# Two transformer blocks in one launch: the opening by channel halves, a new order of panel loads, and block two's side work regrouped among its heads

## The chip, the cores and the metric

One core of one Trainium2 chip runs the whole program in one launch. The metric is the device time in microseconds from the first to the last instruction and what lies around them, as the runs report it; the profile gives the same execution's span. Engines are named as the profile does: PE is the matmul engine (PEld its weight loads), ACT ScalarE, DVE VectorE, POOL GpSimd, SP the engine that only issues DMAs here.

## What is computed

A batch of one, 256 tokens, 1024 channels, float32. The first block:

```python
mod = c @ w_ada + b_ada
shift, scl, gate = split(mod, 3)
h = rms_norm(x, g) * (1 + scl) + shift
u_pool, z_pool, q, k, v, z_attn, m_pool, m_attn = split(h @ w_in)
y_pool = (multiscale_pool(u_pool) * silu(z_pool)) @ w_pool_up
y_attn = (attention(rope(q), rope(k), v) * silu(z_attn)) @ w_attn_up
x = x + gate * ((sigmoid(m_pool) * y_pool + sigmoid(m_attn) * y_attn) @ w_out)
```

The second block takes the normed result. Its modulation (six parts) comes from silu(c_2). It has four retention heads (with a norm over each head and a silu gate), and an attention of eight heads in three branches: over 15 compressed blocks per group of keys and values, over selected blocks, and over a window; each branch is weighted by a sigmoid gate. At 256 tokens the selected and the window branch are two causal softmaxes, so block two has sixteen head passes. The mix goes through w_out_2, and a layer of 16384 small experts (128 x 128 product keys, 16 chosen for each of 8 heads) ends it. With all experts' weights streamed, that layer is 128 panels of `down` and 128 of `up`.

## The kernel before

**Tiles.** Tokens lie in NT = 2 tiles of 128 partitions, channels in C = 8 chunks of 128. A weight panel is 1024 rows by 512 columns, loaded as 128 partitions x 4096 floats in two halves (chunks 0 to 3 and 4 to 7, 1 MB each) into one of SLOTS = 4 slots of SBUF. STREAM (lines 64 to 77) lists the panels in order, each with its user: "pe" panels are multiplied, "dve" panels are modulation columns that DVE sums by itself, "row" is the one modulation panel that PE multiplies as a row. A panel n goes to slot n mod 4, so its load waits until panel n - 4 is used.

**Float32 from three products.** A weight half ("unit", list UNITS, line 90) is split in a high part (ACT's copy to fp32r, `unit_high`, L801, copy at L814) and a low part (POOL's subtraction raw - high, `unit_low`, L735, subtraction at L740, four instructions for a unit; unit 31 alone is DVE's, L1966). The activations are split likewise. PE then adds high x high, low x high and high x low (L1123, L1129, L1135; by rows L1150, L1154, L1163), four matmuls of 512 columns for each token tile in each of the three. HIGH_AT says which of some six places holds the high part of each unit; a place is filled again once the unit before is used.

**Order.** `steps()` (L104) writes out one list of steps, STEPS. Each engine walks through the same list and does its part of each step, so the list's order is the program order of every engine's own queue. POOL is the exception: its units come in the order of UNITS, and the powers for the norms stand between them at fixed places (L757, the retention norm's, behind unit 43). Banks 0 to 3 of PSUM are given out in turn along STEPS (lines 228 to 252); a step that fills a bank waits for the one before to be read.

**Modulation.** A "dve" panel is summed as one `tensor_scalar` (L1663) and seven `scalar_tensor_tensor` (L1665) of 128 x 512, each linked to the one before. Sums with index 0 to 2 (START = 3) accumulate in SBUF (tile tab); those from 3 up to the end of block one accumulate in PSUM and put only the last step in SBUF. PE turns the sum into columns with a product by ones (`start_columns`, L1095, for the first three; L1197 later) or into a row on all partitions for a gate (L1194). DVE's loop sums ahead: behind each "proj" step it does what is due (L2019).

**Opening.** SP loads ada1.2, x, the constants, ada1.3, ada1.0 and ada1.1, then in1.2, the tables and the three broadcast gate rows, then in1.3. DVE sums ada1.2 and ada1.3 (scale), PE makes the row of ada1.0 (`make_row`, L1079, matmuls at L1085), ACT copies it, PE turns it into columns (`row_columns`, L1092), DVE sums ada1.1, and PE turns that into columns. Only when all of scale and shift are there does `mod_ready` rise; then ACT and DVE modulate the four groups of turned chunks (L852, L1735), ACT copies their high parts (L799), DVE subtracts (L1807), and PE starts with in1.2.

**Block one.** Panels in1.4, then 5, 0, 1, 6, 7, 8, 9 one for each attention head; between them score, softmax and product of heads. Then poolup, attnup, out1, and `turn_over(0)` (L138) to block two: the two token tiles are normed, turned and modulated one behind the other, while PE works at out1 and in2.5.

**Block two.** `heads(8, 2 * H, ...)` walks through sixteen head passes with a lag of two: step i has score(8 + i), then the items of list entry i, then the transposes of the head two back, the product of the head three back, then entry i of `small`. DVE masks and takes the maximum (L1709 to L1713), ACT exponentiates (L791), DVE norms the head before (L1726). The items: units of in2.0 to in2.3; `hid`, `hidT`, `cmpK`, `cmpV` (compression network); `cmpS` (scores against compressed keys), `cmpN` (their softmax, twelve small instructions of DVE, L1892 to L1898), `cmpVrep`, `cmpT`, `cmpO`; `ret`, `retO` (retention), `gn` (its statistics, L1997 to L2003), `rn` (its norm, L2008, after POOL's power); `sum` (a step of the gate's modulation panels), `third` (a third of units 40 and 41, which write over the banks that `rn` reads), `gate`, `mT`, `wout_head`.

From 442 us on the expert queries, the selection and the two streamed passes (L1522 to L1526, L1562 to L1568) follow, which the change leaves alone.

## Time and profile before

| what | us |
|---|---|
| median of 3 runs (lowest, highest) | 1271.92 (1267.44, 1272.11) |
| the profiled execution | 1268.93 |
| its span | 1267.1 |
| PE busy | 1193.6 (94%) |
| DVE busy | 904.5 (71%) |
| ACT busy | 619.4 (49%) |
| POOL busy | 551.6 (44%) |

How to read it: the busy share says how much of the span an engine had an instruction running; a busy PE at the lower granted clock gets half as much done. The chain that ended last lies on PE for 75% of the span. The profile's rows name the line, engine, operation, tile written and tile read, with the time that the engine stood idle ahead of an instruction and what released it.

### The profile page before, as it was taken

The numbers are of one execution on the slowest core, as the hardware profiler recorded it, in microseconds if no ns is written. First come the engines' busy times: TensorE is split into PE (matmuls) and PEld (weight loads), VectorE is DVE, ScalarE is ACT, GpSimd is POOL, SyncE is SP. The second block draws the span as 40 slices with busy tenths as digits, with TensorE's granted clock in tenths as the row PEclk, the third lists the DMA queues.
The fourth block names the chain that finished last, engine by engine and source line by source line (L and its number), as shares of the span: only waits on it lengthen the run. The fifth ranks groups of instructions, "written<-read, shape, count | busy, mean of one in ns | idle before, by whom it ended". The sixth has DMA issues, their size and how long they took to land.

```text
span 1267.1 us, 19098 instructions
## 1 busy us (share of the span) xinstructions
PE 1193.6 (94%) x7186; PEld 1050.7 (83%) x7186; DVE 904.5 (71%) x1847; ACT 619.4 (49%) x1077; POOL 551.6 (44%) x323
## 2 busy tenths in 40 slices
PE   4899998899968899999999999999999999999996
PEld 2778876686747699999999999999888888888885
DVE  5678657676685643999948999999566656656566
ACT  2454444444533434444456666555445545444543
POOL 0968759474531202888877777766300000000000
PEclk9899999999978999999999999999999999999998
DMA  9988664354231431565544545455566666666664
GB/s 374 417 329 323 265 266 169 133 206 154 113 150 67 199 133 49 182 184 182 185 160 160 161 156 165 152 153 152 164 231 206 209 231 218 197 185 196 190 196 149
DMA packets 54523, 244.28 MB, mean 193 GB/s; under 512 B 6944, under 2 KB 7328, under 8 KB 42016
## 3 DMA queue, kind: packets, MB, share of 16 engines
q1 hardware_dynamic: 54000, 242.34, 55.4%
q8 instruction: 58, 0.95, 0.3%
q10 hardware_dynamic: 432, 0.72, 0.2%
q14 instruction: 33, 0.27, 0.1%
HBM read 240.94 MB, written 2.10 MB: 192 GB/s over the span
## 4 chain that ended last, share of the span: by engine, by line
PE 75%; DVE 4%; issue 1%; ACT 1%; POOL 0%; POOLq 0%; DVEq 0%; ACTq 0%
PE bank L1526 10%; PE bank L1523 10%; PE bank L1522 10%; PE banks L1562 5%; PE bank L1565 5%; PE bank L1568 5%; PE banks L1565 5%; PE bank L1562 5%; PE banks L1568 5%; PE banks L1536 3%; PE banks L1123 1%; PE banks L1129 1%; PE banks L1135 1%; PE banks L1393 1%; PE banks L1481 1%
## 5 line engine op out<-in xcount | busy, mean ns | idle before, releaser
L765 POOL TENSOR_TENSOR split_r<-ring,split_r 128x1024 fp32r<-128x1024 f32 x128 | 308.0, 2407 | 158.0 <-ACT split_r L996 157.9
L996 ACT ACTIVATE split_r<-ring 128x1024 fp32r<-128x1024 f32 x256 | 269.1, 1052 | 180.2 <-PE bank L1526 180.2
L1522 PE MATMUL bank<-h_high_r,split_r 128*128 128x256 f32 x1024 | 251.3, 283 | 1.7 <-ACT split_r L996 1.7
L1523 PE MATMUL bank<-h_low_r,split_r 128*128 128x256 f32 x1024 | 251.2, 283 | 0.0
L2147 DVE TENSOR_TENSOR split_r<-ring,split_r 128x1024 fp32r<-128x1024 f32 x128 | 156.8, 1225 | 65.6 <-ACT split_r L996 65.6
L1522 PEld LDWEIGHTS bank<-h_high_r,split_r 128*128 128x128 f32 x1024 | 196.3, 192 | 1.9 <-issue 1.9
L1523 PEld LDWEIGHTS bank<-h_low_r,split_r 128*128 128x128 f32 x1024 | 196.4, 192 | 0.0
L740 POOL TENSOR_TENSOR wq_low_r<-G,G_r 128x512 fp32r<-128x512 f32 (+1 forms) x104 | 135.2, 1336 | 68.5 <-ACT G_r L814 68.5
L769 POOL TENSOR_TENSOR small<-small 128x1 f32<-128x1 f32 x2 | 1.5, 760 | 359.0 <-DVE small L2173 359.0
L1526 PE MATMUL bank<-h_high_r,split_r 128*128 128x256 f32 x1024 | 143.7, 283 | 0.2 <-POOL split_r L765 0.2
L1050 ACT ACTIVATE gs_r<-G 128x256 fp32r<-128x256 f32 x128 | 53.5, 418 | 172.5 <-PE bank L1568 172.5
L1526 PEld LDWEIGHTS bank<-h_high_r,split_r 128*128 128x128 f32 x1024 | 132.1, 192 | 0.4 <-POOL split_r L765 0.4
L2095 DVE SCALAR_TENSOR_TENSOR hot_r<-bank,x,w_both_r 128x256 fp32r<-128x256 f32 x256 | 105.5, 473 | 0.0
L2145 DVE TENSOR_TENSOR gs_r<-G,gs_r 128x256 fp32r<-128x256 f32 x128 | 54.3, 424 | 61.8 <-ACT gs_r L1050 61.4
L740 POOL TENSOR_TENSOR wq_low_r<-G,hT_r 128x512 fp32r<-128x512 f32 x48 | 65.3, 1394 | 66.0 <-ACT hT_r L814 66.0
L1562 PE MATMUL banks<-split_r,gs_r 128*128 128x512 f32 x254 | 79.1, 393 | 1.8 <-ACT split_r L996 1.8
L1565 PE MATMUL bank<-split_r,gs_r 128*128 128x512 f32 x254 | 78.2, 389 | 0.0
L1562 PE MATMUL bank<-split_r,gs_r 128*128 128x512 f32 x254 | 78.2, 389 | 0.0
L1568 PE MATMUL banks<-split_r,gs_r 128*128 128x512 f32 x254 | 78.2, 389 | 0.0
L1568 PE MATMUL bank<-split_r,gs_r 128*128 128x512 f32 x254 | 78.2, 389 | 0.0
L1565 PE MATMUL banks<-split_r,gs_r 128*128 128x512 f32 x254 | 78.2, 389 | 0.0
L814 ACT ACTIVATE G_r<-G 128x2048 fp32r<-128x2048 f32 (+1 forms) x26 | 48.7, 1881 | 21.9 <-DMA G<-in_in 18.8
(453 smaller groups left out, 2242.1 us busy)
## 6 DMA issues: line engine op xcount, KB each, us to landing
ring<-in_down SPq DMA_DIRECT2D x128, 512.0 KB, 3.5
ring<-in_up SPq DMA_DIRECT2D x128, 512.0 KB, 3.5
G<-in_ada SPq DMA_DIRECT2D x32, 1024.0 KB, 10.5
G<-in_in SPq DMA_DIRECT2D x32, 1024.0 KB, 7.0
G<-in_out SPq DMA_DIRECT2D x8, 1024.0 KB, 8.1
G<-in_wq SPq DMA_DIRECT2D x8, 1024.0 KB, 7.7
tab<-in_ada SPq DMA_DIRECT2D x4, 1024.0 KB, 5.8
G<-in_poolup SPq DMA_DIRECT2D x2, 1024.0 KB, 6.1
```

Source lines behind the costliest of these rows:

```text
L740: pool.tensor_tensor(low[:, c, :], raw_half[:, c, :], high[:, c, :].bitcast(F32), ALU.subtract)\
L765: pool.tensor_tensor(wsplit[:, j % SPLIT, 1, :], raw[:, j % RAW, :], wsplit[:, j % SPLIT, 0, :].bitcast(F32), ALU.subtract).then_inc(low_r ...
L996: nc.scalar.activation(wsplit[:, n % SPLIT, 0, :], raw[:, n % RAW, :], ACT.Copy).then_inc(high_ready, 1)
L1522: mm(o, w[0][:, c, :], h_high[:, c, :], start=(c == 0), stop=False)
L1523: mm(o, w[0][:, c, :], h_low[:, c, :], start=False, stop=False)
L1526: ins = mm(o, w[1][:, c, :], h_high[:, c, :], start=False, stop=(c == C - 1))
L1562: mm(o, g[0][:, tok], w[:, 0, cols], start=(n == 0), stop=False, skip_group_check=True)
L1565: mm(o, g[1][:, tok], w[:, 0, cols], start=False, stop=False, skip_group_check=True)
L1568: ins = mm(o, g[0][:, tok], w[:, 1, cols], start=False, stop=False, skip_group_check=True)
L2095: ins = stt(out=O2[m % 2][:, t, :, :], in0=iota_p.unsqueeze(1).to_broadcast([P, 2, P]), scalar=picks[:, 1, tok:tok + 1], in1=w_both[:, :, ...
L2145: tt(gs[n % 2][1], Gv[:, n, :], gs[n % 2][0].bitcast(F32), ALU.subtract).then_inc(gs_low, 1)
L2147: tt(wsplit[:, n % SPLIT, 1, :], raw[:, n % RAW, :], wsplit[:, n % SPLIT, 0, :].bitcast(F32), ALU.subtract)\
```

## The change

**Opening by channel halves.** The panels are ada1.2 (scale, first half), ada1.0 (shift, first half), ada1.3 (scale, second half, now the row), in1.2, in1.3, ada1.1 (shift, second half), and from there on "pe" panels come ahead of "dve" panels in each pair. LOADS orders the first halves of in1.2 and in1.3 ahead of ada1.1 and their second halves behind it. Tables come behind the second half of panel 4, gate rows behind panel 8 (with a semaphore of their own, `gates_in`), the band behind panel 10. `mod_ready` now rises for each half. PE makes the row in two halves around `start_columns(1)`, then multiplies in1.2 first half, turns the row and the third sum into columns, and multiplies in1.3 first half, in1.2 second half, in1.3 second half (`in1_products`). UNITS has units 1 and 2 exchanged to match. Two turned groups go to banks 4 and 5. On DVE the step `mods` (third sum, second half of scale and shift) stands behind the first `xsplit`.

**Block one's end.** Since pairs are exchanged, each modulation panel's column product comes one panel later; two instead of one are left behind `y`, and they now stand ahead of the first four `sum` steps. From in1.1 on DVE sums up to four panels ahead instead of three.

**Change of blocks.** `var` of token tile 1 moves ahead of `xlow` and `proj_head`; `low 31` moves ahead of the first in2.5 step.

**Heads of block two.** `cmpS` moves from small entry 6 to 4, `cmpN` from item 7 to 5, `cmpVrep` from 8 to 7, `cmpT` from item 9 to small 8, `cmpO` from item 10 to small 9, `gn` from 10 to 9 (the entry of unit 43's high copy), `rn` from 11 to 10, the thirds, the gate's column product and `gate` one entry earlier each; the sum steps are 2, 3 and 3 at entries 2, 3 and 6 for the first gate panel, and 2, 2, 2, 2 at 11, 12, 13 and 16 for the second.

The core of the diff:

```diff
-STREAM += [("ada1", 2, PANEL, "dve"), ("ada1", 3, PANEL, "dve"), ("ada1", 0, PANEL, "row"), ("ada1", 1, PANEL, "dve")]
-STREAM += [("in1", 2, PANEL, "pe"), ("in1", 3, PANEL, "pe")]
...
+STREAM += [("ada1", 2, PANEL, "dve"), ("ada1", 0, PANEL, "dve"), ("ada1", 3, PANEL, "row"), ("in1", 2, PANEL, "pe"),
+           ("in1", 3, PANEL, "pe"), ("ada1", 1, PANEL, "dve")]
...
+LOADS = [(0, 0), (0, 1), (1, 0), (1, 1), (2, 0), (2, 1), (3, 0), (4, 0), (5, 0), (5, 1), (3, 1), (4, 1)]
+LOADS += [(n, half) for n in range(6, len(STREAM)) for half in range(2)]
...
+UNITS[1:3] = UNITS[2:0:-1]
...
         out.extend([("wout_top", b, 1, 1), ("xT", b + 1, 0, 0), ("xT", b + 1, 0, 1), ("wout", b, 1, 1),
-                    ("rest", b + 1, 0)])
+                    ("rest", b + 1, 0), ("var", b, 1)])
         out.extend(between)
-        out.extend([("var", b, 1), ("norm", b, 1)])
+        out.append(("norm", b, 1))
...
-    ada_after(AT[("in1", 2)], ada)
-    high("in1", 2, (0,))
-    out.extend(("xT", 0, t, half) for t in range(NT) for half in range(2))
-    high("in1", 2, (1,))
-    panel("in1", 2)
+    ada_after(AT[("in1", 4)], ada)
+    out.extend([("xT", 0, 0, 0), ("xT", 0, 1, 0), ("high", 0), ("xsplit", 0), ("row",), ("high", 1), ("high", 2), ("mods",),
+                ("xT", 0, 0, 1), ("xT", 0, 1, 1), ("xsplit", 1), ("high", 3), ("proj", "in1", 2, 0), ("proj", "in1", 2, 1)])
...
-    out.extend(("sum", last, c) for c in range(4))
     for n in ada_after(AT[("poolup", None)], ada):
         out.append(("ada", n))
+    out.extend(("sum", last, c) for c in range(4))
...
-    out.extend([("proj", "in2", 5, 0), ("low", 31), ("proj", "in2", 5, 1)])
+    out.extend([("low", 31), ("proj", "in2", 5, 0), ("proj", "in2", 5, 1)])
...
-        [("unit", 37)] + both(1) + [("high", 38)],
+        [("unit", 37)] + piece(0, 2, 5) + both(1) + [("high", 38)],
         [("hid", 1), ("high", 39)],
-        [("unit", 38)] + piece(0, 2, 4) + [("high", 40)],
-        [("high", 41), ("unit", 39)] + both(2) + piece(0, 4, 6),
-        [("ret", 0), ("ret", 1), ("high", 42), ("cmpN",)],
-        [("retO", 0), ("retO", 1), ("ret", 2), ("ret", 3)] + piece(0, 6, 8),
-        [("cmpT", 0), ("cmpT", 1), ("retO", 2), ("retO", 3), ("high", 43), ("gate_load",)],
-        [("cmpO", 0), ("cmpO", 1), ("gn",)],
+        [("unit", 38), ("cmpN",), ("high", 40)],
+        [("high", 41), ("unit", 39)] + both(2) + piece(0, 5, 8),
+        [("ret", 0), ("ret", 1), ("high", 42)],
+        [("retO", 0), ("retO", 1), ("ret", 2), ("ret", 3)],
+        [("retO", 2), ("retO", 3), ("gn",), ("high", 43), ("gate_load",)],
         [("rn", 0), ("rn", 1)],
-        [("third", 40, 0), ("third", 40, 1)] + piece(1, 0, 2),
-        [("third", 40, 2), ("third", 41, 0), ("ada", gate[0])] + piece(1, 2, 4),
+        [("third", 40, 0), ("third", 40, 1), ("ada", gate[0])] + piece(1, 0, 2),
+        [("third", 40, 2), ("third", 41, 0)] + piece(1, 2, 4),
         [("third", 41, 1), ("third", 41, 2)] + both(3) + piece(1, 4, 6),
-        [("gate", 0)] + piece(1, 6, 8),
+        [("gate", 0)],
         [("gate", 1), ("mT", 1, 0, 0)],
-        [("mT", 1, 1, 0), ("wout_head", 0), ("high", 44)]],
-        {2: [("hidT", 0)], 3: [("cmpK",)], 5: [("rT", 0, 0), ("rT", 0, 1), ("hidT", 1)],
-         6: [("rT", 1, 0), ("rT", 1, 1), ("cmpV",), ("cmpS", 0), ("cmpS", 1)], 8: [("cmpVrep",)]}, 2)
+        [("mT", 1, 1, 0), ("wout_head", 0), ("high", 44)] + piece(1, 6, 8)],
+        {2: [("hidT", 0)], 3: [("cmpK",)], 4: [("cmpS", 0), ("cmpS", 1)],
+         5: [("rT", 0, 0), ("rT", 0, 1), ("hidT", 1)], 6: [("rT", 1, 0), ("rT", 1, 1), ("cmpV",)], 7: [("cmpVrep",)],
+         8: [("cmpT", 0), ("cmpT", 1)], 9: [("cmpO", 0), ("cmpO", 1)]}, 2)
...
             start_columns(0)
...
+            make_row(0)
             start_columns(1)
-            make_row()
-            row_columns()
-            start_columns(2)
+            make_row(1)
...
+            in1_products(2, (0,), True)
+            row_columns()
+            start_columns(2)
+            in1_products(3, (0,), True)
+            in1_products(2, (1,), False)
+            in1_products(3, (1,), False)
...
+                elif kind == "mods":
+                    next_acc()
+                    dve.wait_ge(row_cols, 1)
+                    start_scale(1, ps[7])
+                    dve.wait_ge(start_cols, 3)
+                    start_shift(1, ps[6])
...
-                    ahead = [a for a in ada_steps[:-2] if a[1] < AT[(s[1], s[2])] + 3]
+                    ahead = [a for a in ada_steps[:-2] if a[1] < AT[(s[1], s[2])] + (3 if AT[(s[1], s[2])] < AT["in1", 1] else 4)]
```

`in1_products(i, halves, fill)` is the loop over halves that stood in the "proj" step, with the banks taken at the first half; `make_row(half)` is `make_row` for one half.

## Rows read from the trace of the kernel before

**Rows 1.** The page's part 1: busy us (share), instructions.

```profile
PE 1193.6 (94%) x7186; PEld 1050.7 (83%) x7186; DVE 904.5 (71%) x1847; ACT 619.4 (49%) x1077; POOL 551.6 (44%) x323
```

**Rows 2.** Windows: us, busy us of each engine (instructions), PEclk, DMA share, GB/s.

```profile
16.00:36.00 20.00, 14.09 (x57) 7.77 (x58) 15.16 (x32) 7.11 (x13) 3.64 (x3) 0.96 1.01 420
...
36.00:39.00 3.00, 3.00 (x8) 2.32 (x8) 2.19 (x2) 3.00 (x6) 2.31 (x2) 0.50 1.05 416
...
260.00:263.00 3.00, 3.00 (x14) 3.00 (x14) 2.90 (x8) 0.00 (x0) 3.00 (x3) 0.50 0.97 407
...
285.00:442.00 157.00, 135.16 (x678) 104.74 (x678) 107.27 (x246) 69.14 (x148) 54.37 (x43) 0.91 0.35 136
...
356.00:362.00 6.00, 4.77 (x18) 3.83 (x19) 5.50 (x15) 1.36 (x5) 0.00 (x0) 0.50 0.11 20
...
442.00:1267.00 825.00, 808.73 (x5315) 743.78 (x5314) 599.32 (x1241) 423.74 (x750) 309.50 (x130) 0.99 0.55 175
```

**Rows 3.** Timeline of PE, opening: start, us, what, count [idle ahead <- releaser].

```profile
21.51 1.05 PE L1099 MATMUL banks<-keep,tab 128*128 128x1 f32 x8 [1.34 <-DVE tab L1665]
...
22.49 7.03 PE L1085 MATMUL bank<-G,small 128*1 128x512 f32 x16
...
35.70 3.75 PE L1123 MATMUL bank<-hT_r,ring_r 128*128 128x512 f32 x8 [3.09 <-DVE G L1735]
...
42.05 2.00 PE L1135 MATMUL bank<-wq_low_r,ring_r 128*128 128x512 f32 x8
...
60.85 2.08 PE L1123 MATMUL bank<-G_r,ring_r 128*128 128x512 f32 x8 [0.48 <-issue]
```

**Rows 4.** Timeline of DVE, opening, the third sum.

```profile
25.51 0.48 DVE L1663 TENSOR_SCALAR tab<-G,small 128x512 f32<-128x512 f32 x1 [2.27 <-DMA G<-in_ada]
...
26.03 5.47 DVE L1665 SCALAR_TENSOR_TENSOR tab<-G,small,tab 128x512 f32<-128x512 f32 x7
```

**Rows 5.** Timeline of ACT, opening.

```profile
30.37 1.91 ACT L814 ACTIVATE hT_r<-G 128x2048 fp32r<-128x2048 f32 x1
...
32.97 1.50 ACT L852 ACTIVATE G<-banks,small 128x128 f32<-128x128 f32 x4 [0.68 <-DVEq L1777]
...
34.36 1.15 ACT L799 ACTIVATE ring_r<-G 128x512 fp32r<-128x512 f32 x2
```

**Rows 6.** Timeline of POOL, opening, the first weight unit.

```profile
32.36 5.95 POOL L740 TENSOR_TENSOR wq_low_r<-G,hT_r 128x512 fp32r<-128x512 f32 x4 [17.10 <-ACT hT_r L814]
```

**Rows 7.** Timeline of DVE, sum steps: two rows beside POOL, one without.

```profile
188.72 1.35 DVE L1663 TENSOR_SCALAR tab<-G,small 128x512 f32<-128x512 f32 x1 [0.22 <-DVE G L1918]
...
190.11 5.04 DVE L1665 SCALAR_TENSOR_TENSOR tab<-G,small,tab 128x512 f32<-128x512 f32 x3
...
336.45 1.52 DVE L1665 SCALAR_TENSOR_TENSOR tab<-G,small,tab 128x512 f32<-128x512 f32 x2
```

**Rows 8.** Timeline of DVE and PE, change of blocks.

```profile
242.81 1.23 DVE L1973 TENSOR_TENSOR G_r<-G,ring_r 128x1024 fp32r<-128x1024 f32 x1
...
245.61 0.75 DVE L1622 TENSOR_SCALAR G<-G,small 128x1024 f32<-128x1024 f32 x1 [0.81 <-POOL small L747]
...
259.55 1.14 PE L1154 MATMUL banks<-wq_low_r,ring_r 128*128 128x280 f32 x4 [1.77 <-DVE wq_low_r L1966]
```

**Rows 9.** Timeline of DVE, heads of block two: cmpN's first and last of twelve.

```profile
348.39 0.28 DVE L1892 TENSOR_TENSOR ring<-ring,tab 128x120 f32<-128x120 f32 x1
...
354.72 0.28 DVE L1898 TENSOR_TENSOR ring<-ring,small 128x120 f32<-128x120 f32 x1
```

**Rows 10.** Timeline of PE, heads of block two.

```profile
355.92 0.76 PE L1423 MATMUL bank<-G,tab 15*128 15x128 f32 x2 [4.38 <-DVE ring L1709]
...
376.40 3.78 PE L1123 MATMUL banks<-hT_r,ring_r 128*128 128x512 f32 x8 [4.96 <-DVE ring L2008]
```

**Rows 11.** Timeline of POOL, heads of block two.

```profile
365.51 4.99 POOL L740 TENSOR_TENSOR wq_low_r<-G,G_r 128x512 fp32r<-128x512 f32 x4 [11.30 <-ACT G_r L814]
...
371.79 1.73 POOL L757 TENSOR_TENSOR small<-small 128x8 f32<-128x8 f32 x1 [1.29 <-DVE small L2003]
```

138 lines of the change are left out of this document (74 added, 64 removed).

## The prediction

> **What bounds the kernel now.** I read the page's busy shares first: TensorE works 94% of the span [rows 1]. The windows show where the rest is: 442 to 1267 us, the two expert passes, which no edit touches, leave PE 16 us idle in 825; 285 to 442 us leaves 22 idle in 157, at a mean granted clock of 0.91 [rows 2]. The first products of block one start at 35.70 us [rows 3]. So the change can gain only before 442 us, in what makes PE wait or work at the lower of its two clock levels (share 0.50, 1.2 GHz). All that follows PE in those stages moves with it, and the weights are loaded as PE frees slots, so I carry a delay or gain through to the end one for one. Waits are read from the timelines of the three stages that the diff touches.
>
> **Opening, the front half.** A half panel of 1.05 MB takes 2.49 us at 420 GB/s [rows 2]. The vector engine's third sum began at 25.51 when the first half of panel 3 landed [rows 4]; panel 2's first half is two places ahead, 20.5 us. In the new order PE then makes the first half of the row (half of 7.03 us [rows 3]) to 24.0, start_columns(1) takes 1.05 to 25.1, and shift and scale of the first four chunks are there at 25.3. ScalarE follows with the turn-out (1.50), the high copy of weight unit 0 (1.91; it landed at about 25.4, as seventh panel half) and two part copies (1.15) [rows 5], to 29.9. The first product group starts at 30.0, 5.7 us ahead of before. It also follows closer on seven us of row products. Before, PE started at 1.2 GHz: its first two groups took from 35.70 to 42.05 where the ten from there to 60.37 (60.85 less the 0.48 idle) took 1.83 each [rows 3], and the window shows 0.50 [rows 2]. That is 2.7 us lost.
>
> **Opening, the back half.** Second-half modulation needs the sum of panel ada1.1. It is now in step "mods", behind x0_low of the first half on VectorE: 29.9 plus about 1.7 gives 31.6; its data has landed (30.4 and 32.8). Before, the same eight steps took 6.0 us, from 25.51 to 31.50 [rows 4], with GpSimd idle. GpSimd's first subtraction began at 32.36 [rows 6]; now it begins at 28.9, on the heels of unit 0's high copy, and goes on with units 1 and 2, whose high copies are made by about 32.5 (behind the row's copy) and 37.3 (landing at 35.3): at 6 us each it is busy throughout. What a sum step costs then is shown later: the same form, SBUF operand and SBUF accumulator, took 1.35 for the first and 5.04 for three (1.70 apart) with subtractions running, against 0.76 each (1.52 for two) without [rows 7]. Only the sums from index 3 on accumulate in PSUM; this one, index 2, does not. Eight steps cost 1.4 + 7 x 1.70 = 13.3 us: it ends at 44.9. PE has finished unit 0 and the row's columns by 38, and start_columns(2) is next in its order, ahead of unit 1, so it stands for 7 us. Then 1.05 for the columns, three units of three groups (16.5) and again the 2.7 of the low clock: in1 panel 4 starts at 65.1, where before it started at 60.85. **Opening: 4.2 us lost.** Bounds: with unslowed sums 31.6 + 6.0, no stand of PE and no low clock give 55.2, a gain of 5.7. Taken is the slowed one, because the form and the neighbour on GpSimd are the same.
> The Trainium skill, SBUF — State Buffer, section Who interferes with whom, says that a vector instruction with two SBUF inputs and a GpSimd instruction that reads SBUF exclude each other for the whole instruction. By that rule the trace agrees in kind; a strict alternation of 0.76 with a subtraction of 1.25 would make eight steps 16 us and the opening 7 us worse, where the rows show 1.70 a step.
>
> **Loads.** The gate rows move behind panel 8 and the band behind panel 10. The gate rows (1.5 MB, 4 us) come before panel 9, whose first use is over 10 us off; gateA is first used after in1 panel 5. Panels in1.2 and in1.3 arrive whole by 37.8, before PE wants their second halves. Priced at nothing; if that cover were gone, one half panel late costs 2.5 us. The poolup panel now sits behind ada2.6, 5 us later, with its high copy hidden under in1.9's products (11 us). Each modulation column product comes one panel later; their number is the same. Nothing, between -1 and +1.
>
> **Change of blocks.** Variance of the second token half no longer waits behind x1_low of the first (1.23 at 242.81); the norm at 245.61 [rows 8] had also a trip to GpSimd, now covered by that same subtraction: gain 0.7. low(31) moves ahead of the rope of in2.5: PE had waited 1.77 for it at 259.55 [rows 8], and the window after it is at 0.50 [rows 2], 3 us of work worth 1.5, some 1.7 in all. The rope waits 1.9 instead; its bank is wanted only by in2.4, so next late are VectorE's ropes, under eleven us of PE work. **Gain 4.2**, between 0.7 (something else holds PE there) and 4.5.
>
> **Heads of block two.** The compression softmax, cmpN, ran on VectorE from 348.39 to 355.00, 6.6 us [rows 9], between two heads with little PE work; score masks waited behind it and with them the banks: PE stood 4.4 us ahead of 355.92 [rows 10]; from 356 to 362 it stood another 1.2 and worked the other 4.8 at 0.50 [rows 2], which is 2.4 lost. Now it stands beside unit 38 (three groups, 5.5 us), with cmpS a step earlier still. Gain 8.0 if VectorE keeps up. Given back: (a) the retention norm. gn is now in the same step as high(43), and GpSimd's program has unit_low(43) ahead of the power that gn waits for. Before, the subtractions 365.51 to 370.50 were over when the power ran at 371.79 (1.73), and PE still stood 5.0 ahead of unit 40 at 376.40 [rows 10, 11]. Now high(43) ends some 2 us after gn's inputs are there; subtractions 5.0, power 1.7, norm 2.7 follow in a row, and only two heads' PE work lies between. PE stands about 7: 2.0 given back. The low clock after it stays as before. (b) cmpN, head norms and three sum steps now run while GpSimd subtracts, and retention one head earlier leaves an uncovered score and product at the tail: 0.9. **Gain 5.1**, between -1 (the backlog eats it) and 12 (no stand at unit 40).
>
> **Sum.** +4.2 - 4.2 - 5.1 = -5.1 us. The profiled execution took 1268.9, 1267.1 of it span: it becomes 1263.8. The median of the three runs is 3 us above the profiled one, 1271.9, so the forecast is 1266.8.
>
> **Rivals.** (1) *The opening's sum is not slowed*, because GpSimd starts later or yields: opening -5.7, total -15, 1257. For it: 6.0 us in the trace of before; against it: GpSimd's units have their high copies in time. (2) *The retention norm doesn't wait*: high(43) copies after the statistics' power, or VectorE has slack; heads -10 to -12, total -11, 1261. For it: cmpN, the largest block, is out; against: the program order on GpSimd is fixed. (3) *Slower: VectorE and GpSimd exclude each other.* Price: a sum step of 0.76 behind each subtraction of 1.25 [rows 7, 11] makes 16 us of the sum of ada1.1, over at 47.7, and the opening loses 7; cmpN, norms and sums under subtractions put VectorE some 6 us behind in steps 5 to 8, which turns the heads' gain of 5.1 into a loss of 4; the change of blocks keeps -4.2. Total +7, 1279. It decides from the point where the backlog at the first retention product is over 5 us. (4) *The new order doesn't bring the first products forward*: if the second load queue position or the ScalarE chain puts them past 33 us, nothing changes in kind, since PE would stand for the sum anyway; it is inside the forecast, 1267, and has no chance of its own.
>
> **Chances.** Forecast 0.50 (total -10 to +1), rival 1 0.20, rival 2 0.18, rival 3 0.12. Half a per cent, 6.4 us, is about what a measurement of this kernel can tell from no change. Rivals 1 and 2 lie beyond it, less a few hundredths, and some 0.08 of the forecast too: faster 0.44; same 0.44; slower 0.12. The forecast's own range is 1262 to 1273. The range for 8 in 10 reaches to rival 1 below and near rival 3 above: 1253 to 1276.
>
> **What would show it.** The first L1123-type group starts near 30; VectorE's third sum runs some 13 us with steps of 1.7 beside GpSimd; PE stands about 7 us ahead of the third start_columns and the clock drops after; in1.4 starts near 65. No PE wait on low(31). In the heads no stand at cmpVrep; a wait of the retention norm on GpSimd's power right behind unit_low(43). The prediction is wrong if the third sum ends before 40, or if unit 40 starts less than 20 us after the score of head 15.

## The result and the profile after

The changed kernel takes **1300.3 us** (median of 4 runs, 1298.54 to 1300.79), the kernel before on the same chip 1270.62: a ratio of 1.0242, 95% interval [1.0223, 1.0261]. It is 30 us slower. The forecast was 1266.8 in 1253 to 1276, with 0.12 on slower. The profiled execution took 1300.79, 1299.0 of it span. Of the runs behind the experiments below, two of the ten with one sum less ahead took 1539 and 2376 us and stand outside the ratios.

The page's part 1 and windows, the latter with the columns of [rows 2]:

```profile
PE 1209.7 (93%) x7186; PEld 1060.7 (82%) x7186; DVE 905.4 (70%) x1847; ACT 618.7 (48%) x1077; POOL 552.4 (43%) x323
```

```profile
36.00:42.00 6.00, 3.06 (x16) 2.36 (x16) 5.86 (x5) 0.79 (x1) 6.00 (x4) 1.00 1.01 420
42.00:53.00 11.00, 8.10 (x24) 6.77 (x25) 8.12 (x13) 4.35 (x7) 7.44 (x6) 0.53 0.23 93
115.00:230.00 115.00, 92.33 (x422) 76.65 (x421) 55.64 (x110) 36.15 (x54) 57.04 (x46) 0.84 0.52 209
...
324.00:472.00 148.00, 131.21 (x668) 101.02 (x669) 102.79 (x241) 67.24 (x143) 53.57 (x43) 0.93 0.36 139
```

Instructions are the same in number. PE is busy 16 us longer with as many of them: more of its work runs at the half clock. The place is 115 to 230 us, block one: 22.7 us idle and a mean granted clock of 0.84, where the kernel before, from 115 to 175 us, has PE busy for 60.00 of 60 at 1.00:

```profile
115.00:175.00 60.00, 60.00 (x313) 50.47 (x313) 41.85 (x75) 25.12 (x38) 40.08 (x32) 1.00 0.71 283
```

The heads of block two, on the other hand, take 148 us where they took 154.5, less idle and at 0.93 for 0.91.

To find each stage's share I read the start of one and the same instruction in both timelines of PE (us; the last column is what the stage between two rows gave or took):

| start of | before | after | difference | of this stage |
|---|---|---|---|---|
| head 0, score | 75.57 | 79.72 | +4.15 | opening +4.2 |
| head 3, score | 115.26 | 120.06 | +4.80 | +0.6 |
| head 7, score | 174.70 | 206.53 | +31.82 | **block one +27.0** |
| first product with out1 | 213.22 | 254.04 | +40.83 | **behind head 7 +9.0** |
| head 8, score | 285.55 | 323.98 | +38.43 | change of blocks -2.4 |
| first product of the expert stage | 440.05 | 472.02 | +31.97 | heads -6.5 |
| end of span | 1267.1 | 1299.0 | +31.9 | -0.1 |

Of the three parts that I priced, the opening and the heads came out near their price and the change of blocks at 2.4 us of 4.2. The loss is in two stages that I had priced at nothing. In the timeline of PE of the kernel after, the start, a group's busy time, and in brackets the idle time ahead of it:

```profile
30.40 2.08 PE L1128 MATMUL banks<-hT_r,ring_r 128*128 128x512 f32 x8 [1.39 <-ACT ring_r L802]
...
44.90 1.87 PE L1104 MATMUL bank<-keep,tab 128*128 128x1 f32 x8 [5.84 <-DVE tab L1683]
...
65.84 2.06 PE L1128 MATMUL banks<-G_r,ring_r 128*128 128x512 f32 x8
...
125.62 2.05 PE L1128 MATMUL banks<-G_r,ring_r 128*128 128x512 f32 x4 [4.65 <-issue]
...
147.87 0.95 PE L1339 MATMUL bank<-ring,G 128*128 128x256 f32 x2 [4.36 <-DVE small L1715]
...
169.35 2.04 PE L1350 MATMUL bank<-ring 128*128 128x128 f32 x8 [3.60 <-DVE small L1712]
...
191.57 3.75 PE L1128 MATMUL banks<-G_r,ring_r 128*128 128x512 f32 x8 [4.64 <-issue]
...
212.14 1.09 PE L1074 MATMUL bank<-keep,G 128*128 128x128 f32 x4 [4.11 <-DVE small L1715]
```

The first three rows answer to [rows 3]: products start at 30.4 in place of 35.7, PE stands (waits with nothing to run) for the third sum, in1.4 starts at 65.84 in place of 60.85. The other five are new: one stand of 3.6 to 4.65 us in each in1 panel from head 3 on. After each, PE works at the half clock: four products of 512 columns take 2.05 us in place of 1.1, and the windows of 4 to 5 us behind the stands show a granted clock of 0.50 to 0.59. What the stands wait for is seen on VectorE:

```profile
117.52 0.75 DVE L1683 SCALAR_TENSOR_TENSOR tab<-G,small,banks 128x512 f32<-128x512 f32 x1
119.16 0.76 DVE L1681 TENSOR_SCALAR banks<-G,small 128x512 f32<-128x512 f32 x1 [0.90 <-PE bank L1222]
...
124.70 0.75 DVE L1683 SCALAR_TENSOR_TENSOR tab<-G,small,banks 128x512 f32<-128x512 f32 x1
125.37 0.15 DVE L1715 TENSOR_TENSOR small<-bank,small 128x4 f32<-128x4 f32 x1
...
140.20 0.76 DVE L1681 TENSOR_SCALAR banks<-G,small 128x512 f32<-128x512 f32 x1 [12.18 <-PE bank L1222]
...
147.66 0.16 DVE L1715 TENSOR_TENSOR small<-bank,small 128x4 f32<-128x4 f32 x1
```

At 117.52 to 118.27 one sum ends; at 119.16 VectorE, in its program order, starts the next, as soon as PE has made the column product (L1222) that frees the accumulator. From then on each sum waits for that product, 12.18 us at 140.20. Behind the sum in VectorE's queue stand the add that empties the column product's bank (L1715) and the head's mask. PE needs the bank, and its next product starts at 125.62, right behind that add. The sums have caught up with the products that free their two accumulators. The source shows why at four and not at three. The number is a distance in the list of panels, in which PE's and VectorE's panels take turns: three reaches the next sum, four also the one after it. That one needs the accumulator whose column product stands in PE's order right behind the very panel that PE is multiplying.

The rows of the other stages, PE, then GpSimd and VectorE in block two:

```profile
286.91 0.66 PE L1074 MATMUL banks<-keep,G 128*128 128x128 f32 x4 [2.23 <-DVE G L1640]
...
306.90 1.20 PE L1159 MATMUL banks<-wq_low_r,ring_r 128*128 128x512 f32 x4 [1.04 <-POOL wq_low_r L745]
...
407.22 3.78 PE L1128 MATMUL banks<-hT_r,ring_r 128*128 128x512 f32 x8 [4.92 <-DVE ring L2036]
```

```profile
397.96 4.93 POOL L745 TENSOR_TENSOR wq_low_r<-G,G_r 128x512 fp32r<-128x512 f32 x4 [5.43 <-ACT G_r L817]
402.85 1.64 POOL L762 TENSOR_TENSOR small<-small 128x8 f32<-128x8 f32 x1
...
404.52 2.64 DVE L2036 TENSOR_SCALAR ring<-banks,small 128x128 f32<-128x128 f32 x8 [0.83 <-POOL small L762]
```

### The profile page after: what moved, and what is told of

The parts are those of the page before. It is cut to its first block, busy times and chain, and to the rows that moved or that the text cites. A ratio compares the mean times of both kernels' runs of the same rounds, so it can differ in the third digit from the quotient of the medians.

```text
span 1299.0 us, 19103 instructions
## 1 busy us (share of the span) xinstructions
PE 1209.7 (93%) x7186; PEld 1060.7 (82%) x7186; DVE 905.4 (70%) x1847; ACT 618.7 (48%) x1077; POOL 552.4 (43%) x323
## 4 chain that ended last, share of the span: by engine, by line
PE 87%; DVE 5%; issue 2%; POOL 2%; ACT 2%; DMA 1%; SPq 1%; POOLq 0%; DVEq 0%; ACTq 0%
PE bank L1544 9%; PE bank L1541 9%; PE bank L1540 9%; PE banks L1580 4%; PE bank L1583 4%; PE bank L1586 4%; PE banks L1583 4%; PE bank L1580 4%; PE banks L1586 4%; PE banks L1128 4%; PE banks L1134 3%; PE banks L1140 3%; PE banks L1554 3%; POOL wq_low_r L745 1%; PE bank L1128 1%
```

## The experiments

Two theories stood after this; each recorded text below says what each would give. **A**: the loss is the sums' order alone; from in1.1 on they go one step too far ahead. **B**: it comes from the exchange of the panels in each pair (loads, banks, the place of the column product). Ratios are against the kernel before on the same chip. Fourteen kernels ran.

**One sum less ahead, all else as after.**

```diff
-                    ahead = [a for a in ada_steps[:-2] if a[1] < AT[(s[1], s[2])] + (3 if AT[(s[1], s[2])] < AT["in1", 1] else 4)]
+                    ahead = [a for a in ada_steps[:-2] if a[1] < AT[(s[1], s[2])] + 3]
```

> The changed kernel with one number put back: VectorE sums modulation panels three ahead everywhere, not four from in1.1 on. Theory A (the lead): in the changed kernel VectorE, behind the second token tile of in1.1, 6, 7, 8 and 9, waits for the column product of the sum two back, which stands in PE's queue behind that very panel; the sum of 6.3 us then stands ahead of the next score mask, and PE waits 3.6 to 4.7 us five times and works on at the lower clock. With three ahead the first four of these waits go and the last stays (two sums are due at in1.9): the score of head 6 stands within 8 us of before's 160.9 (changed kernel: 186.0), and the time falls by 22 to 30 us, to 1270 to 1278. Theory B (the exchanged panel order): panels or banks come late because pairs are exchanged and gate rows and band moved; then the lead changes little, under 5 us, and the waits stay.

Measured: 1273.89, ratio 1.0034 [1.0018, 1.0049]. The four stands from 125 to 192 us are gone; head 7 starts 4.77 us behind the kernel before, as head 3 does. These remain in the timeline of PE:

```profile
185.09 1.08 PE L1074 MATMUL bank<-keep,G 128*128 128x128 f32 x4 [4.10 <-DVE small L1715]
...
208.99 1.56 PE L1128 MATMUL banks<-G_r,ring_r 128*128 128x512 f32 x4 [2.51 <-DVE G L1962]
...
226.90 2.08 PE L1155 MATMUL bank<-hT_r,G_r 128*128 128x512 f32 x4 [1.80 <-DVE ring_r L2013]
```

Of the 2.42% that the change costs, that one number is 2.08, or 26 us.

**The same number alone in the kernel before**, its pairs in the old order.

```diff
-                    ahead = [a for a in ada_steps[:-2] if a[1] < AT[(s[1], s[2])] + 3]
+                    ahead = [a for a in ada_steps[:-2] if a[1] < AT[(s[1], s[2])] + (3 if AT[(s[1], s[2])] < AT["in1", 1] else 4)]
```

> The kernel before with the lead alone raised to four from in1.1 on, nothing else. Theory A: the same waits appear in the old order, since there too the column product of the sum two back stands behind the panel: PE waits some 4 us at each of in1.1, 6, 7 and 8 and the time rises by 20 to 30 us, to 1291 to 1300. Theory B: no change, within 3 us.

Measured: 1295.68, ratio 1.0223 [1.0188, 1.0258]. The same stands come up in the old order (4.64, 4.35, 3.60 and 4.65), the first two being:

```profile
120.48 3.75 PE L1123 MATMUL banks<-G_r,ring_r 128*128 128x512 f32 x8 [4.64 <-issue]
...
142.60 1.00 PE L1321 MATMUL bank<-ring,G 128*128 128x256 f32 x2 [4.35 <-DVE small L1692]
```

So the lead makes the loss in either order, and with either opening. Theory B is out for block one up to head 7; behind head 7 this run loses nothing (38.5 us to the first product with out1, as before), so the 9 us there are not the lead's.

**Change of blocks and heads of block two on the kernel before**, opening and block one untouched: the change's own edits of `turn_over`, of the in2.5 line and of the list of the heads.

```diff
-                    ("rest", b + 1, 0)])
+                    ("rest", b + 1, 0), ("var", b, 1)])
...
-        [("cmpO", 0), ("cmpO", 1), ("gn",)],
+        [("retO", 2), ("retO", 3), ("gn",), ("high", 43), ("gate_load",)],
...
```

> The kernel before with the regrouped heads of block two and the two moved steps in the change of blocks, opening and stream as before. By the two traces the heads gained 6.5 us (score 8 to the expert queries 154.5 before, 148.0 after) and the change of blocks 2.4 (first out product to score 8: 72.3 before, 69.9 after). If the parts add: 8.9 us faster, 1262. Rival: these gains were there only because the kernel came in late, with its loads long landed; then under half of it, under 4 us.

Measured: 1262.32, ratio 0.995 [0.9935, 0.9966]; from head 8 to the expert stage 148.3 us where the kernel before takes 154.5. By these two executions the heads are worth 6.2 us. The whole is 6 us faster and not the 8.9 of the theory, though its 1262 was met: the theory had counted from a slower run of the kernel before. The rival's under 4 is out.

**Change of blocks alone.**

```diff
-                    ("rest", b + 1, 0)])
+                    ("rest", b + 1, 0), ("var", b, 1)])
...
-        out.extend([("var", b, 1), ("norm", b, 1)])
+        out.append(("norm", b, 1))
...
-    out.extend([("proj", "in2", 5, 0), ("low", 31), ("proj", "in2", 5, 1)])
+    out.extend([("low", 31), ("proj", "in2", 5, 0), ("proj", "in2", 5, 1)])
```

> The kernel before with only the two moved steps of the change of blocks: variance of the second token half ahead of the subtraction of the first, and the subtraction for unit 31 ahead of the rope. My prediction said 4.2 us gained (0.7 of the norm, 1.8 of PE's wait for unit 31, 1.7 of the low clock behind it). The two traces say 2.4. If the first: score 8 at 281.4 and 1267; if the second: score 8 at 283.2 and 1268.5; the wait of PE on VectorE for unit 31 is gone either way, and what is left tells whether the clock or another wait took its place.

Measured: 1268.1, ratio 0.999 [0.9975, 1.0004], no difference. The wait for low 31 went, and the next user of GpSimd's low parts waits in its place, one unit later:

```profile
269.77 1.20 PE L1154 MATMUL bank<-wq_low_r,ring_r 128*128 128x512 f32 x4 [1.22 <-POOL wq_low_r L740]
```

From head 0 to head 8 it is 1.05 us shorter than before; in the next run, where nothing in that stretch is changed, 0.62 us shorter. What is left is half a microsecond here. In the two versions with both regroupings on the old opening the stretch is 1.22 and 2.62 us shorter than before, so single profiles size this edit no closer than that.

**The compression's norm alone.**

```diff
-        [("unit", 38)] + piece(0, 2, 4) + [("high", 40)],
+        [("unit", 38), ("cmpN",)] + piece(0, 2, 4) + [("high", 40)],
...
-        [("ret", 0), ("ret", 1), ("high", 42), ("cmpN",)],
+        [("ret", 0), ("ret", 1), ("high", 42)],
...
-        {2: [("hidT", 0)], 3: [("cmpK",)], 5: [("rT", 0, 0), ("rT", 0, 1), ("hidT", 1)],
-         6: [("rT", 1, 0), ("rT", 1, 1), ("cmpV",), ("cmpS", 0), ("cmpS", 1)], 8: [("cmpVrep",)]}, 2)
+        {2: [("hidT", 0)], 3: [("cmpK",)], 4: [("cmpS", 0), ("cmpS", 1)], 5: [("rT", 0, 0), ("rT", 0, 1), ("hidT", 1)],
+         6: [("rT", 1, 0), ("rT", 1, 1), ("cmpV",)], 8: [("cmpVrep",)]}, 2)
```

> The kernel before, with one thing alone: the compression's scores move to item 4 and its norm to item 5 of the heads of block two; the retention's order, the gate row's sum and everything else stay. Prediction's theory (the stand of TensorE behind cmpN was worth 8.0 us): about 1262 us, the 6.63 us stand ahead of unit 40 down to under 2 us. Rival A (the stand is set by more than cmpN: the retention's norm, which is still last, holds the same engine): 1265 to 1268, a stand of 4 us or more before the products of unit 40. Rival B (the norm lands on the rest of VectorE's work at item 5 and delays a head's mask): 1270 or more, with a new stand between scores 13 and 15.

Measured: 1265.62, ratio 0.9973 [0.9958, 0.9987], rival A in time and in kind, its stand of 4 us or more being 3.85. The timeline of PE:

```profile
344.54 0.48 PE L1281 MATMUL bank<-G 64*128 64x128 f32 x2 [1.74 <-ACT ring L922]
...
355.47 0.49 PE L1281 MATMUL bank<-G 64*128 64x128 f32 x2 [2.02 <-DVE ring L1911]
...
372.35 3.78 PE L1123 MATMUL banks<-hT_r,ring_r 128*128 128x512 f32 x8 [3.85 <-DVE ring L2008]
```

The stands of 4.38 and 4.96 us [rows 10] became 1.74, 2.02 and 3.85. The stage is 3.8 us shorter (4.1 by the medians), half of my 8.0; the score ahead of which VectorE was busy now has two smaller stands. (The text before the run gave the stand ahead of unit 40 as 6.63 us. That is the row of the version with both regroupings; before it is the 4.96 of [rows 10].)

**GpSimd's power ahead of the low part of unit 43**, on the version with both regroupings.

```diff
-            for u in range(34, 44):
+            for u in range(34, 43):
                 unit_low(u)
             pool.wait_ge(gn_var, 1)
             pool.tensor_tensor(rr, cs, half_neg, ALU.pow).then_inc(gn_rstd, 1)
-            for u in range(44, 46):
+            for u in range(43, 46):
```

> The kernel with the new change of blocks and the new order of the heads on the old opening, and GpSimd's power for the retention moved ahead of the low part of unit 43. The prediction priced that order at 2.0 us of retention norm behind unit_low(43); by that: 2.0 us under the same kernel without the move (1262.3), 1260.3. By the trace of the changed kernel the power started only 1.6 us after the statistics it needs, and the norm waited 0.83 us for it: 1261.5, that is no difference that can be measured. Rival: the stand before unit 40 is set by VectorE's own queue, then nothing changes at all and that stand stays at 5 us or more.

Measured: 1261.6, ratio 0.9945 [0.9927, 0.9963], not told apart from the 1262.32 without. GpSimd's row moved from 365.99 to 361.81, the products of unit 40 from 370.41 to 369.88:

```profile
361.81 1.64 POOL L757 TENSOR_TENSOR small<-small 128x8 f32<-128x8 f32 x1 [6.37 <-DVE small L2003]
```

```profile
369.88 3.78 PE L1123 MATMUL banks<-hT_r,ring_r 128*128 128x512 f32 x8 [4.66 <-DVE ring L2008]
```

GpSimd is 4 us earlier and PE half a microsecond. The norm (L2008) had waited 1.53 us for the power in the version without (367.71); here it starts right behind VectorE's own norm of a head, at 367.19. So with the power out of the way VectorE's own queue holds it. The stand of 4.66 lies a little under the 5 us or more that the rival had named.

**The opening's third sum in PSUM**, with one sum less ahead.

```diff
-                part = ps[4 + k % 2][:, :] if START <= k < BLOCK_ONE else a
+                part = ps[4 + k % 2][:, :] if START <= k < BLOCK_ONE else ps[7][:, :] if k == 2 else a
...
-                    ins = mm(ps[7][:, c:c + 1], row[:, c * P:(c + 1) * P], ones[0:1, 0:1], start=True, stop=True)
+                    ins = mm(ps[6][:, 8 + c:9 + c], row[:, c * P:(c + 1) * P], ones[0:1, 0:1], start=True, stop=True)
...
                     dve.wait_ge(row_cols, 1)
-                    start_scale(1, ps[7])
                     dve.wait_ge(start_cols, 3)
+                    start_scale(1, ps[6][:, 8:12])
                     start_shift(1, ps[6])
```

> The kernel after with the lead of the sums back at three, and the third column sum of the opening accumulated in a PSUM bank in place of SBUF (its shift and scale columns go to another bank). If the third sum is slow because VectorE and GpSimd both work in SBUF (prediction's opening term: steps of 1.65 beside GpSimd against 0.78 in PSUM): the steps fall to about 0.8, the 5.84 us stand ahead of its column product falls under 0.5, the low clock behind it goes with it, and the time is 8 to 9 us under the 1273.9 of the same kernel without the move: about 1265. Rival (the sum is slow for another reason, for instance the loads that land in its panel, or GpSimd slows it wherever it accumulates): steps stay over 1.4 us and the time stays at 1272 to 1275.

Measured: 1263.75, ratio 0.996 [0.9945, 0.9974], by the two ratios 9.4 us under the run with the smaller lead alone; head 0 starts 8.5 us earlier (71.22 against 79.74). First the third sum and GpSimd beside it in the kernel after, then in this one:

```profile
31.57 1.52 DVE L1681 TENSOR_SCALAR tab<-G,small 128x512 f32<-128x512 f32 x1
33.12 11.72 DVE L1683 SCALAR_TENSOR_TENSOR tab<-G,small,tab 128x512 f32<-128x512 f32 x7
35.87 12.56 POOL L745 TENSOR_TENSOR wq_low_r<-G,G_r 128x512 fp32r<-128x512 f32 x8
```

```profile
30.70 0.74 DVE L1681 TENSOR_SCALAR bank<-G,small 128x512 f32<-128x512 f32 x1
31.48 4.71 DVE L1683 SCALAR_TENSOR_TENSOR bank<-G,small,bank 128x512 f32<-128x512 f32 x6
...
34.37 9.98 POOL L745 TENSOR_TENSOR wq_low_r<-G,G_r 128x512 fp32r<-128x512 f32 x8
```

A step of the sum falls from 1.67 to 0.79 us and a subtraction of GpSimd from 1.57 to 1.25. The stand of 5.84 us is gone. That both engines gain from it shows that they held each other up while both worked in SBUF; whether by the reads or by the writes was not separated. The Trainium skill, SBUF — State Buffer, Who interferes with whom, says that a vector instruction with at most one SBUF input, outside its 2-port modes, doesn't contend with GpSimd, and that one with two does where GpSimd reads SBUF; by that rule, the trace agrees in which form is slowed. Its "exclusive lock" for a whole instruction would give 0.76 + 1.25 = 2.0 us a step, where this trace shows 1.67.

**The last two pairs in the old order**, on top of the last one (and with the power ahead), to take the sum away that follows head 7.

```diff
-             (("in1", 6), ("ada2", 0)), (("in1", 7), ("ada2", 1)), (("in1", 8), ("ada2", 8)), (("in1", 9), ("ada2", 9))):
+             (("in1", 6), ("ada2", 0)), (("in1", 7), ("ada2", 1)), (("ada2", 8), ("in1", 8)), (("ada2", 9), ("in1", 9))):
```

> The version that the runs so far point to: the kernel after with a lead of three, the third sum in PSUM, the last two pairs of block one's panels in the old order (sum's panel first, so that one sum less falls between the last head and the change of blocks), and the power before unit_low(43). Theory (block one's lost time is the sums' order alone): waits of 4.10, 2.51 and 1.80 us behind head 7 are gone or under 1 us, the change of blocks starts 13 us earlier than with the lead of three alone, and the time is 1255 to 1258. Rival (the time behind head 7 is lost to the gates' later load or to the new bank order, not to the sums): those waits stay and the time is 1263 to 1266, what the third sum alone gives.

Measured: 1269.64, ratio 0.9999 [0.9986, 1.0013], 6 us slower than without it, outside both expectations. Behind head 7 the stand of 4.10 is gone (one of 1.18 is left), but two came up ahead of it:

```profile
146.55 2.04 PE L1350 MATMUL bank<-ring 128*128 128x128 f32 x8 [3.60 <-DVE small L1712]
...
168.54 2.04 PE L1128 MATMUL banks<-G_r,ring_r 128*128 128x512 f32 x4 [3.94 <-DVE small L1712]
```

Where the order turns, two modulation panels follow each other, so VectorE is given two sums in a row, and the second waits for a product that stands one panel on. It is the same fault as the lead of four, made by the order of the panels: with the new order throughout (the run before) and with the old one throughout (below) these stands are not there.

**The lead of four, and the column product one panel earlier.**

```diff
-        sums = ada_after(AT[(name, i)], ada)
+        sums = ada_after(AT[(name, i)] + 2 * (name == "in1"), ada)
```

> The kernel after, lead of four and new panel order kept, with one thing alone: TensorE's column product of a sum is issued behind the in1 panel that precedes the sum's panel in the new order, one in1 panel earlier than in the kernel after, which is where it stood in the kernel before. Theory (sums run two ahead of products, so each accumulator is freed too late): all five waits of 3.6 to 4.65 us in block one go and the y region's with them, the last head of block one starts 4 to 5 us behind the kernel before, and the time is 1264 to 1268, near the number of the prediction. Rival (the sums' panels are loaded too late for a lead of four in the new order, and the product's place only shifts the wait): VectorE then waits for its panels' loads, TensorE for VectorE's columns, and the time is 1275 or more.

Measured: 1276.37, ratio 1.0054 [1.0037, 1.007]. The time is the rival's (1275 or more), and VectorE does wait for its panels' loads, 5.36 us at 150.63 and 3.57 at 167.89, but PE does not stand there. In PE the theory holds for the most part. Of the five stands four are gone; one, of 3.35, is left at the turn from three to four, where VectorE makes two sums in a row, and the mask and the bank's emptying wait behind them:

```profile
115.13 0.74 DVE L1681 TENSOR_SCALAR banks<-G,small 128x512 f32<-128x512 f32 x1
...
121.32 0.75 DVE L1681 TENSOR_SCALAR banks<-G,small 128x512 f32<-128x512 f32 x1
...
127.52 0.15 DVE L1715 TENSOR_TENSOR small<-bank,small 128x4 f32<-128x4 f32 x1
```

```profile
127.77 3.63 PE L1128 MATMUL bank<-G_r,ring_r 128*128 128x512 f32 x8 [3.35 <-issue]
```

So the distance between a sum and the product two back is what matters, from whichever side it is set right: 24 us came back here, 26 with the smaller lead. Behind head 7 this version loses 3.2 us in place of 9, since one product less is left over there.

**The same with the third sum in PSUM and the power ahead.**

> The same with the third sum of the opening in PSUM and the power ahead of unit_low(43). Theory: the gains add, 10.1 us for the third sum as between the two runs with a lead of three, nothing for the power: 1255 to 1258, the fastest of all. Rival (with the opening 9 us shorter, the loads become what bounds block one, and the gain is given back there): the heads of block one start with new waits for panels, time 1260 to 1266.

Measured: 1267.51, ratio 0.9983 [0.9969, 0.9998]; the opening gives 9 us, and the stand at the turn stays. Neither text had that: by the ratios it is 3 us over the one with the smaller lead; the stand at the turn (3.13 here) and the 3.2 us behind head 7 are what the trace shows for it.

**Old pairs throughout, new opening.** Sum's panel first again, lead of three, third sum in PSUM, both regroupings, power ahead.

```diff
-for a, b in ((("in1", 4), ("ada1", 4)), (("in1", 5), ("ada1", 5)), (("in1", 0), ("ada2", 2)), (("in1", 1), ("ada2", 3)),
+for a, b in ((("ada1", 4), ("in1", 4)), (("ada1", 5), ("in1", 5)), (("ada2", 2), ("in1", 0)), (("ada2", 3), ("in1", 1)),
...
-    ada_after(AT[("in1", 4)], ada)
+    ada_after(AT[("ada1", 4)], ada)
```

> The kernel after from the fourth in1 panel on with the old order of panels, sums and products (sum's panel first, lead of three), the new opening kept with its third sum in PSUM, the new change of blocks and heads kept, and the power ahead of unit_low(43). Theory (the 6 us that the version with a lead of three loses between head 7 and the end of the change of blocks come from the one sum that the new order puts behind head 7): the waits of 4.10 and 1.54 us behind head 7 go, and from head 7 to the end it takes as long as the kernel before with the two regroupings. But panel in1.4 now lands one panel, 5 us, later: first product of in1.4 0 to 5 us later than with the lead of three and PSUM. Sum: 1255 to 1260. Rival (those 6 us are the later load of the gates or the banks): the waits stay and the time is 1262 to 1268.

**In1.4 ahead of its sum's panel**, else the same: only this one pair is left in the new order.

```diff
+STREAM[6:8] = STREAM[7:5:-1]
...
-        sums = ada_after(AT[(name, i)], ada)
+        sums = ada_after(AT[(name, i)] + 2 * ((name, i) == ("in1", 4)), ada)
```

> The same, but panel in1.4 is loaded ahead of the two sums' panels that follow it, and the column product of the first of these sums is issued right behind in1.4; from in1.5 on all is as in the old order. Theory: in1.4 starts as early as with the lead of three and PSUM (55 to 57 us), the two sums in a row on VectorE are covered there, since no head waits for VectorE yet, and the time is 0 to 4 us under that of the old pairs: 1254 to 1257. Rival (two sums in a row keep VectorE from the rotary work on the q and k panels and the wait only moves to the first scores): the first score starts 3 us or more later than with the lead of three and PSUM, and the time is 1258 to 1264.

Measured: 1267.39, ratio 0.9985 [0.997, 0.9999], and 1266.76, ratio 0.9983 [0.9971, 0.9995]. The first time is its rival's, though the theory's stands behind head 7 did go; the second is over both of its texts. In the first the 4.10 behind head 7 is 1.18, and from head 7's score to head 8's it takes 109.5 us where the new pairs with the same lead take 116.8: the sum left behind head 7 was worth 7.3 us. The gain was lost again ahead of head 0, which starts at 78.97 against 71.22. PE and ScalarE there:

```profile
75.40 1.94 PE L1074 MATMUL banks<-keep,G 128*128 128x128 f32 x8 [4.57 <-ACT G L884]
```

```profile
70.38 1.91 ACT L817 ACTIVATE G_r<-G 128x2048 fp32r<-128x2048 f32 x1 [11.40 <-DMA G<-in_in]
72.86 1.91 ACT L817 ACTIVATE hT_r<-G 128x2048 fp32r<-128x2048 f32 x1 [0.56 <-DMA G<-in_in]
74.68 1.06 ACT L884 ACTIVATE G<-banks 128x512 f32<-128x512 f32 x2
```

ScalarE empties in1.4's bank (L884) only behind the high copies of in1.5, and that panel lands behind the three gate rows, whose later place I had priced at nothing. In the kernel after, the load queue works 0.23 of the time from 42 to 53 us: panels wait for slots there, the gate rows need none.

**Gate rows into that gap**, in each of the two.

```diff
-                if (n, half) == (2 * SLOTS, 1):
+                if (n, half) == (6, 1):
                     sp.dma_start(gateA, d["gate1"].partition_broadcast(P)).then_inc(gates_in, 16)
```

> The version with the new opening and the old pairs, with the three gate rows loaded right behind panel 6 in place of behind panel 8, where the load queue stands idle from 46 to 52 us. Theory (their place holds back panel in1.5, its high copy on ScalarE and behind it the copy of in1.4's bank): in1.5 lands 5 us earlier, the stand of 4.57 us ahead of the second transposes of q and k goes, the first score starts near 74 us in place of 79, and the time is 5 us under the version without: 1261 to 1263. Rival (VectorE's sum ahead of the second rotation holds the transposes): stand and time stay, 1266 to 1268.

> The version with in1.4 ahead of its sum's panel, the gate rows loaded right behind panel 6. Theory: as above the stand of 5.73 us goes, first score near 73 to 74 us, time 5 us under the version without: 1260 to 1262. Rival (two sums in a row on VectorE hold the transposes or the first mask): a stand of 3 us or more ahead of the transposes or the second score stays, 1265 to 1267.

Measured with the old pairs: **1259.0**, ratio 0.9926 [0.9909, 0.9942], the fastest of all and by the two ratios 7.5 us under the version without (theory: 5). ScalarE's copies come 4.2 us earlier and the stand is gone:

```profile
68.64 1.92 ACT L817 ACTIVATE hT_r<-G 128x2048 fp32r<-128x2048 f32 x1 [0.56 <-DMA G<-in_in]
70.47 1.06 ACT L884 ACTIVATE G<-banks 128x512 f32<-128x512 f32 x2
```

Head 0 starts at 73.86 (5.1 us earlier), head 1 at 86.65 (7.7 earlier: the half clock behind the stand went with it). With in1.4 ahead: 1264.75, ratio 0.9963 [0.995, 0.9976]. By the ratios that is 2.5 us under the version without. Its stand ahead of the second transposes shrank from 5.73 to 0.78, but another of 3.37 follows it, for a bank (the gate row's product) that VectorE empties behind two sums in a row. That was its rival, in part. Two sums in a row cost something even where no head waits.

## Why the prediction was wrong

**The step that failed** is the order of VectorE's sums and their column products in block one, which the sum has at nothing. It failed in two places. The lead of four, one edited number of the diff, has no term at all and no reason for having none. And "Loads" says: "Each modulation column product comes one panel later; their number is the same. Nothing, between -1 and +1." I counted products and not distances. The sum of panel k may begin only when the product of panel k-2 has been issued, and I didn't ask what an earlier sum or a later product keeps waiting. The chain was there to be found in the source: sum, bank-emptying add and mask in VectorE's order, bank in PE's. The lead cost 27 us up to head 7, shown by both halves of the test: taking the lead back gives 26 us back, and the lead alone costs the kernel before 27 (1295.68 against 1268.37). Another 9 us went behind head 7, and the lead has no part in them: with a lead of three and the new pairs that stage still loses 8.9 us, with the lead of four and the old pairs nothing, with a lead of three and the old pairs 1.3. They are the one sum and product that the exchanged pairs leave over there, as the run with the product one panel earlier bears out (3.2 lost). That is the line on the loads ("one panel later"), at nothing.

Both signs by which I would have called the prediction wrong stayed on its side: the third sum ended at 44.8 and not before 40, and unit 40 started 25.65 us after the score of head 15 and not less than 20. Neither looked at block one.

**Opening, +4.2: right in each term of the kernel after; the 4.2 also rests on which execution of the kernel before it is held against.** First products forecast for 30.0, measured 30.40; third sum 1.4 + 7 x 1.70 = 13.3 us, measured 1.52 + 11.72; its end 44.9 forecast, start_columns(2) at 44.90; stand 7 forecast, 5.84 measured; half clock after it, 0.53 in the window; in1.4 at 65.1 forecast, 65.84 measured. That the contention in SBUF is the cause is shown by the run with PSUM. It also sizes rival 1, "not slowed": I had 9.9 us between the two, and it gave 8.5 at head 0 and 9.4 by the ratios. But an unchanged opening brings head 0 anywhere from 75.2 to 79.5 us (last section), and the kernel before was read in an early one (75.57); against the latest, the new opening at 79.7 loses next to nothing.

**Loads, the gate rows at nothing: right for this order of panels only.** The trace of the kernel after, whose in1.5 comes ahead of them, shows no wait for their place, though it was not tried there by itself; it was worth 7.5 us once the pairs stood in the old order, and 2.5 with in1.4 ahead. I did not say that the price holds for one order.

**Change of blocks, -4.2: over-sized.** The stage is 2.4 us shorter in the kernel after, but also 1.8 in the run where only the compression's norm was moved and 1.5 in the one where only the lead was, so that much comes without the edit. The edit alone gave about half a microsecond in its profile and, by the medians, nothing that can be told from zero. The 1.77 us for low 31 I counted as gained; in the traces a wait of 1.22 (edit alone) or 1.04 us (kernel after) for the same GpSimd takes its place one unit on. The next late one was GpSimd's following low part, not VectorE's ropes.

**Heads, -5.1: near in sum (6.5 and 6.2 measured), wrong in parts.** The compression's norm was 3.8 and not 8.0, since the smaller stands that it had covered come up. The 2.0 to be given back for GpSimd's order was not: the norm waited 0.83 us for the power (1.53 in the version without the new opening), and the power 4 us earlier changes nothing that the times can tell. PE stood 4.92 ahead of unit 40 [rows 10 has 4.96], not 7.

**Rival 3** named the side that came, for another mechanism: it came to +7 us in all by VectorE and GpSimd excluding each other. Their contention is real, but it was already in the forecast's opening; the loss in block one has nothing of it, since the sums that wait there accumulate in PSUM and take 0.79 us a step (4.71 for six).

## What to carry to other kernels

Where a producer fills one of two buffers and a consumer on another engine frees them, write down for each place in the order how many fills ahead and how many frees behind stand there, before and after the edit. A count that reaches the number of buffers turns independent work that is queued behind the producer into a stand per round (here 5 of some 4.3 us, each followed by the half clock), and an edit of the lead, of the producer's place or of the consumer's place does it alike. Look for gaps of a load queue that waits for slots and put loads there that need none. A term priced at nothing deserves the same working as the others, and the two regroupings alone (6 us) would have been the better change.

## What the runs showed of the hardware

**The clock fell with no idle stretch right ahead of it.** In the kernel after (windows, then the timeline of PE):

```profile
223.00:226.60 3.60, 3.60 (x31) 3.34 (x29) 2.21 (x4) 2.29 (x2) 3.60 (x4) 1.00 0.00 0
226.60:230.00 3.40, 3.40 (x12) 2.92 (x12) 3.12 (x6) 0.00 (x0) 3.40 (x3) 0.51 0.00 0
```

```profile
226.20 1.41 PE L1222 MATMUL banks<-keep,tab 128*128 128x1 f32 x8
227.46 2.05 PE L1128 MATMUL banks<-hT_r,ring_r 128*128 128x512 f32 x4
```

From 223.0 to 226.6 PE has 3.60 us busy of 3.60, with products of 128 x 64 and 128 x 1 at full clock; the next products, 128 x 512, run at the half clock. The last idle time ahead of that, 1.31 us, ends at 214.54. A stretch that is busy by the profile was followed by the low level all the same. No run was made on this alone, so its cause stays open.

**The half clock adds half again to a stand.** The four stands between heads 3 and 7 add up to 17.3 us (4.65 + 4.36 + 3.60 + 4.64), and that stretch lost 27.0; the other 9.8 are work at the lower level behind each of them.

**The opening of an unchanged kernel comes out up to 4.3 us apart.** Head 0 starts at 75.57 us in the kernel before and at 75.21, 75.79, 77.91, 77.94 and 79.53 in the five versions that leave its opening alone. In the three late ones the second column product takes 1.86 or 1.87 us in place of 1.05 and the row behind it 8.4 to 10.0 in place of 7.0, so that the first product of in1.2 starts at 37.2 to 38.8 and not at 35.2 to 35.7. The granted clock that the profile gives from 20 to 30 us is 1.00 in all six, so what slowed these products stays open. Later stages that an edit leaves alone move too, though less: the heads of block two take 153.2 to 155.8 us in the three profiles with the old list, the change of blocks 70.6 to 72.3. A part of one or two microseconds read from one profile of each kernel is therefore not told from nothing; the 27 and the 9 us are.
